# Expert weights in 2 MB DMAs of 16 KB rows, with two more pairs of slots ahead of the first expert

## The reference

```python
cap = EC_CAPACITY * s // N_EXPERTS                 # 2 * 256 // 16 = 32 tokens per expert
vals, idx = lax.top_k(jnp.swapaxes(probs, 1, 2), cap)
xe = jax.vmap(lambda hb, ib: hb[ib])(h, idx)
a = jnp.einsum('becd,edf->becf', xe, w_gate_e)     # w_gate_e: 16 x 1024 x 2048
u = jnp.einsum('becd,edf->becf', xe, w_up_e)       # w_up_e:   16 x 1024 x 2048
y = jnp.einsum('becf,efd->becd', jax.nn.silu(a) * u, w_down_e)   # 16 x 2048 x 1024
```

## Time and profile before

| | us |
|---|---|
| median of 3 runs | 1432.08 (1430.69 to 1432.92) |
| the profiled execution, its time | 1429.03 |
| its span, first to last instruction | 1427.2 |
| PE busy in the span | 1162.0 (81%) |
| head, until the first expert product | 278.2 |
| experts, from there to the end of the last down product | 922.2 |
| tail, the rest of the span | 226.8 |

### The profile page before, as it was taken

How to read it: one execution, slowest core, us unless ns; L and a number is a source line. 1 busy time by engine, 2 the same in 40 slices (tenths; PEclk the granted TensorE clock), 3 DMA queues, 4 the chain that set the end, 5 groups by cost and what they waited for, 6 DMA issues and landing times.

```text
span 1427.2 us, 16989 instructions
## 1 busy us (share of the span) xinstructions
PE 1162.0 (81%) x7070; PEld 634.3 (44%) x7071; DVE 322.9 (23%) x459; ACT 246.1 (17%) x355; POOL 87.7 (6%) x95
## 2 busy tenths in 40 slices
PE   4999999888778787777777778777787777996888
PEld 1789999533323133131222213213122223996777
DVE  1546446310000000000000000000000002666555
ACT  2423533100000000000000000000000003653644
POOL 2000000000000000000000000000000001421122
PEclk8999999697887968978787896888868889998989
DMA  9996884599999999999999999999999999742311
GB/s 333 379 361 240 265 299 174 228 421 421 422 422 421 422 421 422 422 422 422 422 422 422 422 422 422 422 422 422 422 422 422 422 422 373 242 143 89 119 64 55
DMA packets 116634, 496.33 MB, mean 348 GB/s; under 512 B 8140, under 2 KB 60772, under 8 KB 64116
## 3 DMA queue, kind: packets, MB, share of 16 engines
q1 hardware_dynamic: 114944, 490.37, 86.2%
q0 software_dynamic: 1296, 5.19, 1.1%
q10 hardware_dynamic: 356, 0.21, 0.1%
HBM read 494.70 MB, written 1.05 MB: 347 GB/s over the span
## 4 chain that ended last, share of the span: by engine, by line
DMA 45%; PE 36%; SPq 8%; DVE 4%; ACT 4%; issue 2%; POOL 0%; DVEq 0%; ACTq 0%
DMA ring<-in_w_gate_e 28%; SPq L463 8%; DMA ring<-in_w_down_e 8%; DMA ring<-in_w_up_e 7%; PE psum L556 7%; PE psum L557 6%; PE psum L558 6%; PE psum L823 6%; PE psum L804 4%; DMA ring<-in_w_in 3%; PE psum L850 2%; PE psum L624 1%; ACT ring_r L1035 1%; ACT arena L1165 1%; PE psum L675 1%
## 5 line engine op out<-in xcount | busy, mean ns | idle before, releaser
L823 PE MATMUL psum<-ring,arena 128*32 128x512 f32 x2048 | 314.6, 735 | 118.2 <-DMA ring<-in_w_gate_e 72.8
L850 PE MATMUL psum<-ring,arena 128*32 128x512 f32 x1024 | 233.0, 696 | 52.9 <-DMA ring<-in_w_down_e 38.8
L823 PEld LDWEIGHTS psum<-ring,arena 128*32 128x32 f32 x2048 | 57.3, 124 | 346.2 <-DMA ring<-in_w_gate_e 152.4
L850 PEld LDWEIGHTS psum<-ring,arena 128*32 128x32 f32 x1024 | 55.8, 121 | 220.9 <-DMA ring<-in_w_down_e 113.7
L556 PE MATMUL psum<-ring_r,ht_hi 128*128 128x256 f32 (+1 forms) x384 | 114.9, 299 | 10.9 <-DVE ht_lo L1289 7.8
L1285 DVE TENSOR_TENSOR ring_r<-ring,ring_r 128x2048 fp32r<-128x2048 f32 x43 | 101.9, 2394 | 74.0 <-ACT ring_r L1035 73.9
L556 PE MATMUL psum<-ht_hi,ring_r 128*128 128x256 f32 x384 | 109.3, 285 | 6.1 <-issue 6.1
L558 PE MATMUL psum<-ring_r,ht_lo 128*128 128x256 f32 (+1 forms) x384 | 113.2, 295 | 0.0
L557 PE MATMUL psum<-ring_r,ht_hi 128*128 128x256 f32 (+1 forms) x384 | 112.8, 294 | 0.0
L804 PEld LDWEIGHTS psum<-arena 128*128 128x128 f32 x544 | 99.9, 288 | 25.7 <-issue 24.7
L1035 ACT ACTIVATE ring_r<-ring 128x2048 fp32r<-128x2048 f32 x55 | 103.1, 1907 | 47.6 <-DMA ring<-in_w_in 30.5
(11 more groups left out here) (255 smaller groups left out, 958.0 us busy)
## 6 DMA issues: line engine op xcount, KB each, us to landing
ring<-in_w_gate_e SPq DMA_DIRECT2D x128, 1024.0 KB, 26.5
ring<-in_w_up_e SPq DMA_DIRECT2D x128, 1024.0 KB, 26.9
ring<-in_w_down_e SPq DMA_DIRECT2D x128, 1024.0 KB, 26.9
ring<-in_w_in SPq DMA_DIRECT2D x38, 1024.0 KB, 11.2
ring<-in_w_ada SPq DMA_DIRECT2D x24, 1024.0 KB, 11.0
ring<-in_w_conv_out SPq DMA_DIRECT2D x4, 1024.0 KB, 6.0
ring<-in_w_o SPq DMA_DIRECT2D x4, 1024.0 KB, 11.1
ring<-in_w_out SPq DMA_DIRECT2D x4, 1024.0 KB, 4.8
```

Source lines behind the costliest of these rows:

```text
L823: last = mm(psum[32 * g:32 * g + 32, b, :], cur[h][:, k, :], slot_in(s, g=4, n=512)[:, g, :], start=(k == 0), stop=(k == KD - 1), tile_pos ...
L850: last = mm(psum[32 * q:32 * q + 32, 2 + n, :], act_t[:, f % 4, (f // 4) * CAP:(f // 4 + 1) * CAP], w[:, kk, n * BANK:(n + 1) * BANK], sta ...
```

## The change

Expert slots now come in pairs: one DMA of 2 MB fills two neighbouring places, with 16 KB in one piece per partition. For that the row layout changes. Gate and up pairs take rows `(p k)` with k = 2: partition p gets rows 2p and 2p + 1 of 256 rows. Down pairs take k = 4 of 512 rows. So token columns are taken with stride 2 wherever they meet those rows: `pairwise()` in the transposes of `x`, of two modulation vectors, in the gather, and in the router weights. Three small vectors (`vec3`) are loaded once more in that order by ACT and transposed apart. The activation is transposed with stride 4 instead of 2.

A second tensor, `extra`, holds two pairs (4 slots, 32 KB per partition) on memory that in the head is `gfin` and working areas. It takes slots 16 to 19 of the first expert, once. Slots 20 and up use the ring again: the previous owner of slots 20 to 35 is 20 slots back, and later it is 16 back as before; SP waits until both slots of the previous pair are used up. To free that memory `xt` moves into `xr`, `mix_tmp` shrinks from four buffers to one (with a wait of DVE on its own previous addition), the squares of L1118 are written elsewhere (with a wait of ACT on its own previous one), and `gfin` is loaded after the extra pairs are used up. The first two experts stand unrolled ahead of the loops of SP and PE, which have 7 turns.

```diff
@@ block.sync @@
-            with sp.Fori(0, NE // 2) as i:
-                for h in range(2):
-                    for j in range(EXPERT_SLOTS):
-                        s = HEAD_SLOTS + h * EXPERT_SLOTS + j
...
-                        if j < 16:
-                            src = w[:, (j % 8) * P:(j % 8 + 1) * P, :].rearrange("e (k p) n -> p (e k) n", p=P)
-                        else:
-                            src = w[:, (j - 16) * 2 * P:(j - 15) * 2 * P, :].rearrange("e (p k) n -> p (e k) n", p=P)
-
-                        before = HEAD_RING if s < HEAD_SLOTS + HEAD_RING else RING
-                        sp.wait_ge(slot_used, 2 * EXPERT_SLOTS * i + (s - before + 1))
...
+            def load_pair(i, e):
+
+                h, j = divmod(e % (2 * EXPERT_SLOTS), EXPERT_SLOTS)
...
+                rows, k = (2 * P, 2) if j < 16 else (4 * P, 4)
+                first = (j % 8) // 2 * rows
+                src = w[:, first:first + rows, :].rearrange("e (p k) n -> p (e k) n", k=k)
+                at = expert_place(e)
+                to = extra[:, at - RING:at - RING + 2, :] if at >= RING else ring[:, at:at + 2, :]
+                sp.dma_start(shaped(to.rearrange("p a b -> p (a b)"), k=k, n=src.shape[2]), src).then_inc(loaded[at], 16)
...
+            for d in range(4):
+                sp.wait_ge(slot_used, HEAD_SLOTS - HEAD_RING + 2 * d + 2)
+                load_first(d)
+            sp.wait_ge(z_ready, 4)
+            sp.wait_ge(gate_row_done, 4)
+            for d in range(PAIRS, PAIRS + EXTRA):
+                load_first(d)
+            for used, d in ((2, 4), (2, 6), (4, 5), (4, 7)):
+                sp.wait_ge(slot_used, HEAD_SLOTS - WO + used)
+                load_first(d)
+            for e in range(2 * (PAIRS + EXTRA), 2 * EXPERT_SLOTS, 2):
+                sp.wait_ge(slot_used, HEAD_SLOTS + released(e))
+                load_pair(0, e)
+            with sp.Fori(1, NE // 2) as i:
+                for e in range(2 * EXPERT_SLOTS, 4 * EXPERT_SLOTS, 2):
+                    sp.wait_ge(slot_used, 2 * EXPERT_SLOTS * i + (HEAD_SLOTS - 2 * EXPERT_SLOTS + released(e)))
+                    load_pair(i, e)
@@ block.gpsimd @@
-            await_bank(pool, "head", head_u["seq23"], 1)
-            pool.dma_start(gfin, t["g_final"].partition_broadcast(P)).then_inc(side_loaded, 16)
...
             take_weigh(1, 1)
+            pool.wait_ge(slot_used, HEAD_SLOTS + RING + 2 * EXTRA)
+            pool.dma_start(gfin, t["g_final"].partition_broadcast(P)).then_inc(side_loaded, 16)
@@ block.tensor, gather and expert @@
-                        last = mm(bank(2)[:, k * CAP:(k + 1) * CAP], x[:, tt, k * P:(k + 1) * P], pick_cur[h][:, tt, :],
+                        last = mm(bank(2)[:, k * CAP:(k + 1) * CAP], pairwise(x[:, tt, :], k), pick_cur[h][:, tt, :],
...
+                    at = expert_place(e)
+                    if e % 2 == 0:
+                        p, n = landing[HEAD_SLOTS + e]
+                        pe.wait_ge(loaded[p], 16 * n if first else 48 * i + (16 * n - 48))
...
-                        last = nc.tensor.transpose(bank(0, c=4, m=P)[:, c, :], act_h.rearrange("q (b p k) -> q b p k", b=2, k=2)[:, c // 2, :, c % 2], ident)
+                    last = nc.tensor.transpose(bank(0, c=4, m=P)[:, c, :], act_h.rearrange("q (p k) -> q p k", k=4)[:, :, c], ident)
```

More of the change, by code:

```diff
@@ L260, in build @@
         router_loaded, gate_bias_loaded = sem("router_loaded"), sem("gate_bias_loaded")
-        loaded = [sem(f"slot{p}_loaded") for p in range(RING)]
+        loaded = [sem(f"slot{p}_loaded") for p in range(RING)] + [sem(f"extra{p}_loaded") for p in range(2 * EXTRA)]
         slot_used = sem("slot_used")
@@ L630, in turn_modulation @@
                 for c in range(4):
-                    last = nc.tensor.transpose(bank(to, c=4, m=P)[:, c, :], mod_rows[b][:, c * P:(c + 1) * P], ident)
+                    rows = pairwise(mod_rows[b], c) if b else mod_rows[b][:, c * P:(c + 1) * P]
+                    last = nc.tensor.transpose(bank(to, c=4, m=P)[:, c, :], rows, ident)
                 last.then_inc(mod_turned, 1)
@@ L641, in _ @@
                     pe.wait_ge(vec_loaded, 16 * VEC_DMAS)
-                    nc.tensor.transpose(psum[:, 7, P:2 * P], vec1, ident).then_inc(vec_turned, 1)
+                    nc.tensor.transpose(psum[:, 7, P:2 * P], vec1, ident)
+                    for j in range(2):
+                        last = nc.tensor.transpose(psum[:, 7, 2 * P + 16 * j:2 * P + 16 * j + 12], pairwise(vec3[0:12, :], j), ident[0:12, 0:12])
+                    last.then_inc(vec_turned, 1)
                 if k == 6:
@@ L861, in _ @@
+            for h in range(2):
+                expert(0, h, first=True)
+            with pe.Fori(1, NE // 2) as i:
+                for h in range(2):
+                    expert(i, h)
             pe.wait_ge(side_loaded, 32)
@@ L1056, in _ @@
             s = first_slot["fourier_in"]
-            first, half = ring[:, place(s)[0], :], SLOT // 2
+            first, half = ring[:, place(s), :], SLOT // 2
             arrived(act, s)
```

193 lines of the change are left out of this document (113 added, 80 removed).

## The result

The changed kernel takes **1414.03 us** in the median of 4 runs (1413.32 to 1414.80), the kernel before 1431.38 us beside it: a ratio of 0.988, with a 95% interval from 0.9868 to 0.9892. The prediction was 1413.6 us. The profiled execution of the changed kernel took 1413.32 us, with a span of 1411.2 (before: 1429.03 and 1427.2).

The account below looks back on a forecast made before the run. The prediction took the stream of weights by DMA as the bound. Its terms, -9.9 - 13.1 + 1.7 + 1.5 + 1.3 = -18.5 us, gave 1413.6 us from the median of 1432.08; 80% range 1404 to 1428.

Parts of the forecast that it names:

- Rival D: Expert stage: TensorE becomes the bound if its mean clock falls from 0.83 to about 0.68; chance 2%.
- Part 1: Head: four more slots on chip before the weight stream starts, 2.485 us each, gain 9.9 us, down to 5.
- Rival B: Head: extra slots land after 280 us or the first gather slows; 5 to 8 us lost, 1419 to 1422; chance 8%.
- Part 2: Weight stream: 16 KB pieces take a pair from 4.970 to 4.898 us, over 182 DMAs a gain of 13.1 us.
- A: Weight stream: piece size brings nothing, a pair stays at 4.970 us, 1426.7 us in all; chance 18%.
- C: Weight stream: bigger pieces are slower, a pair over 4.970 us; 1444.8 us at 414 GB/s; chance 5%.
- E: Weight stream: more gain than the line gives, 434.6 GB/s and 1400 us; chance 5%.
- Part 3: Stream's start and end: what loading in pairs costs, +1.7 and +1.5 us; waits in between cost nothing.
- (a): Stream start: the first load now needs two used slots, +1.7 us, range 0.2 to 1.9.
- (b): Stream end: PE has two slots left after the last landing, 1.91 us more, ACT covers 0.4: +1.5 us.
- Part 4: `g_final`, 512 KB, moves from the head into the full stream: +1.3 us; other moved loads and waits taken as 0.
- Strided reads: Gather ahead of the first expert and activation transposes: strided sources cost 0 to +1.9 us, taken as 0.

Follow-up runs that it names:

- experiment 4: Changed kernel without the two extra pairs, so slots 16 to 19 go through the ring; pieces stay 16 KB: 1423.56 us, ratio 0.9948.
- experiment 1: Changed kernel with each pair loaded by two DMAs of 1 MB, pieces of 8 KB again: 1427.59 us, ratio 0.9971.
- experiment 6: Changed kernel with the first ring pair in two DMAs, the first megabyte sent once one slot is used: 1411.13 us, ratio 0.9855.
- experiment 9: Changed kernel with the first ring pair in two DMAs and `g_final` loaded when all but the last expert slot are used: 1410.39 us, ratio 0.9851.
- experiments 1 to 5: Includes three more variants of the changed kernel: 2 MB DMAs with 8 KB pieces (1427.49 us), with 4 KB pieces (1453.93), `g_final` loaded four slots before the end (1413.63).
- Experiment 10: As experiment 9, plus the last pair of every second expert in two DMAs of 1 MB: 1413.40 us, ratio 0.9862.
- 8: Changed kernel with `g_final` four slots before the end, first ring pair split, and last pair of every second expert split: 1411.43 us, ratio 0.9853.

## Why the prediction was right

**The bound** was read rightly: the stream took nearly what was predicted of it. From the first product to the landing of the last weights the terms give -9.9 - 13.1 + 1.7 + 1.3 = -20.0, and it measured 920.26 - 900.12 = -20.1. PE waits more for DMA than before, in 680 us instead of 700 (total us, times, longest):

```profile
PE psum L904 <- DMA ring<-in_w_down_e: 76.2, 42, 3.0
PE psum L878 <- DMA ring<-in_w_gate_e: 62.0, 29, 3.0
PE psum L878 <- DMA ring<-in_w_up_e: 38.0, 21, 3.0
```

Rival D, TensorE as the bound, had 176 us of distance here, at a clock of 0.80.

**Part 1, the four slots, -9.9.** 9.75 by experiment 4's last pair, 9.5 by the medians. The forecast times of the issues fit too: 233.75 for "233", and the last slots landed at 270.3, with 8.7 us to spare. Rival B is out.

**Part 2, 16 KB pieces, -13.1.** 182 x (4.970 - 4.894) = 13.8 by the profile, and 13.6 between the medians of experiment 1 and the changed kernel. The line through 8 KB and 1 KB, 9.0 ns a piece and 0.0368 ns a byte, was 0.004 us a pair too high, 0.7 us in all, and it holds at 4, 16 and 32 KB. The step that was a risk was that a line through two points, from different stages, says something of a third beyond both; three more points now lie on it. Rivals A, C and E are out by 428 GB/s. What the Trainium skill (DMA: Bandwidth & Descriptors, Latency and other measured facts) says for C, that partitions at large powers of two apart lose rate, doesn't show at a distance of 16 KB, nor at 32 KB with 431 GB/s; its own cases begin at 512 KB, where it has 207 GB/s of a full 214, and reach half the rate only at 4 MB. No run here touches those.

**Part 3.** (a) The wait for the second slot: the first ring load is at 282.73 - 279.02 = 3.71 us behind the first product instead of 280.21 - 278.23 = 1.98. That is +1.7 as priced for the start. How much of it reaches the end is less sure: when it was undone alone, the last weights landed 0.4 us earlier (experiment 6). (b) The end of a pair: from the last landing (1179.14) to `ht_hi` it takes 11.0 us, from the last slot's landing before 9.9. **+1.2 instead of +1.5**, but the step behind the 1.5 was wrong, and the size is near by luck. I had held that a second slot costs PE 1.91 us more. At full clock it costs 0.03, since the pair's products run four at a time and not two (1.94 us against 1.91). What cost 1.4 us here was the clock: PE had 0.50 at the last pair and took 3.30 us for it. ScalarE now waits 1.04 us for PE where it waited not at all. In experiments 6 and 9, whose profiles have the full clock there, the landing is 9.6 and 9.8 us ahead of `ht_hi`, no more than before. So the end of a pair costs nothing at full clock and 1.2 us at half clock. In the profiles of the changed kernel (both) and of experiments 1 to 5 PE had the half clock for most of the last pair, in those of 6 and 9 the full one; whether the split of the first pair brings that about or chance does isn't shown. Experiment 10 shows the cover's other side: let `g_final` get in the way of the next transfer and ScalarE's split is what `ht_hi` waits for.

**Part 4, `g_final`, +1.3.** By the last landing experiment 9 against 6 has 1.8 us for it, 10 against 8 has 1.0; 0.52 MB at 428 GB/s are 1.2. Right within about half a microsecond, which is what the stretch of one kernel differs by between two executions.

**Strided reads, 0.** The gather takes 7.05 us before and after. From 400 to 1080 us its weight loads are not slower either, and those of the activation's transposes, at stride 4 now, take 211 ns in the mean where stride 2 had 216 (columns: busy, mean ns of one | idle before; the first two lines are before, the others now):

```profile
L804 PEld LDWEIGHTS psum<-arena 128*128 128x128 f32 x352 | 64.8, 288 | 17.2 <-issue 17.2
L837 PEld LDWEIGHTS psum<-arena 128*128 128x128 f32 x48 | 8.4, 216 | 26.1 <-DVE arena L1526 26.1
L855 PEld LDWEIGHTS psum<-arena 128*128 128x128 f32 x352 | 54.9, 246 | 15.0 <-issue 15.0
L892 PEld LDWEIGHTS psum<-arena 128*128 128x128 f32 x45 | 6.7, 211 | 22.4 <-DVE arena L1597 22.4
```

By the rule of two hits per cacheline in the Trainium skill (SBUF — State Buffer, Specifications (TRN2)) stride 4 should pay where stride 2 doesn't; these rows show no difference that counts.

**What was off.** The rate gave 0.7 us more than predicted, and between first product and last landing about 0.6 us more were lost elsewhere, which I can't name. The result is -17.4 by the medians against -18.5; the predicted time is only 0.4 us off because the kernel before also measured 0.7 lower this time (1431.38 and not 1432.08). The difference of 1.1 isn't in a term of the sum: the profile has +0.8 in the head and +2.1 in the tail, both of which the changed kernel has in one execution and less or otherwise in another, and I had no term for how much PE's clock moves between executions. And one number of "what would show it" contradicted its own sum: "the last down product 22 to 23 us earlier, at about 1176" left out the +1.7 and the +1.3, with which it is 20.0 earlier, at 1178.5. It was 19.3 earlier, at 1179.19.

## What to carry to other kernels

Where the DMA engines are busy all the time, ask how long a single contiguous piece is and not how large the DMA: here each piece costs 9 ns on its engine beside its bytes, so 4, 8, 16 and 32 KB give 409, 422, 428 and 431 GB/s, and one DMA of 2 MB instead of two of 1 MB gives nothing. Two piece sizes in one trace, each in a full queue, were enough here to price a third. In a kernel that streams at its bound, a byte that is on chip before the stream starts, or that is moved behind its end, is worth about its full transfer time. A bigger unit delays the start, since more places must be free (1.7 us here; splitting the first unit brought 0.4 of it back at the end). Whether it also costs at the end must be read from how the products of one unit overlap: here a pair took TensorE no longer than one slot at the same clock. Compare two variants by a mark that TensorE's clock doesn't move, such as the last landing. A load on another queue doesn't wait behind a full queue but takes its share at once, so "late" has to mean behind the last landing, and behind what the tail waits for next.

## What the runs showed of the hardware that I had not expected

- A DMA as such costs almost nothing in a full queue: a 1 MB DMA alone takes 4.8 us from issue to landing, but twice as many of them for the same pieces change the rate by nothing (422 and 422 GB/s).
- TensorE's drops to half its clock, in stretches of little work, last 6.8, 10.2 or 13.7 us at the same place of the same tail; one kernel had 13.7 in one execution and 10.2 in the next, where a third drop was missing too, 1.5 us of its end in all, and over all kernels the tail differs by 3.8 us. A difference of 2 us between two profiles is not evidence for anything before these stretches are compared.
- The clock at a single place can decide what a small change seems to bring: the same 16 products of the last pair took 3.30 us at 0.50 and 1.94 us at 1.00, and that alone was 1.25 of the 1.64 us between the stretches of experiment 6 and the changed kernel.
- TensorE works through products of different column groups side by side: 8 down products on two groups took 1.91 us and 16 on all four took 1.94, both at full clock.
